# Attention product with the values as the stationary operand, in a hybrid encoder layer on one core

## The reference, cut to what matters

```python
def window_sink_attention(q, k, v, sinks):
    ...
    scores = jnp.einsum('bnqkgd,bnskd->bnkgqs', q, k_band).astype(jnp.float32) * (ATT_HEAD_DIM ** -0.5)
    scores = jnp.where(valid[None, :, None, None, None, :], scores, -jnp.inf)
    sink = sinks.astype(jnp.float32).reshape(1, 1, ATT_KV_HEADS, ATT_GROUP, 1)
    lse = jnp.logaddexp(jax.nn.logsumexp(scores, axis=-1), sink)
    probs = jnp.exp(scores - lse[..., None]).astype(v.dtype)
    out = jnp.einsum('bnkgqs,bnskd->bnqkgd', probs, v_band)
    return out.reshape(b, s, ATT_Q_W)

def hybrid_mixer(h, w_in, b_in, w_qk_conv, b_qk_conv, sinks, g_att, g_ml, w_out):
    ...
    att = rmsnorm(att, g_att)
    ml = rmsnorm(ml.reshape(b, s, ML_HEADS, ML_V_DIM), g_ml.reshape(ML_HEADS, ML_V_DIM)).reshape(b, s, ML_V_W)
    return jnp.concatenate([att, ml], axis=-1) @ w_out
```

## Time and profile before

| what | value |
|---|---|
| median of 3 runs | 1009.53 us (1009.29 to 1009.66) |
| profiled execution | 1009.17 us |
| its span | 1007.4 us |
| PE busy | 997.8 us, 99% of the span |
| DVE, ACT, POOL busy | 744.7, 505.8, 25.9 us |
| granted TensorE clock | 0.999 of full speed, mean |

### The profile page before, as it was taken

The page is one execution under the profiler, slowest core; times in us unless marked ns, Lnnn a source line. Parts: engine busy times, 40 slices in busy tenths (PEclk is TensorE's granted clock), DMA queues, the critical chain, the costliest instruction groups (busy, mean ns, idle before and its releaser), DMA issues.

```text
span 1007.4 us, 13062 instructions
## 1 busy us (share of the span) xinstructions
PE 997.8 (99%) x4807; PEld 823.8 (82%) x4807; DVE 744.7 (74%) x1164; ACT 505.8 (50%) x949; POOL 25.9 (3%) x40
## 2 busy tenths in 40 slices
PE   9999999999999999999999999999999999999997
PEld 6788888888888888788888888888888888888886
DVE  4563678875645569997777777777776879996796
ACT  5663448643733225755445445445544634444573
POOL 2000000000300000000000000000000000000000
PEclk9999999999999999999999999999999999999999
DMA  9527554222832241423223223223222999035104
GB/s 343 186 91 224 187 189 168 85 66 108 298 117 84 84 124 51 141 84 105 63 84 104 63 84 104 63 84 100 68 81 81 391 363 336 1 117 190 40 1 167
DMA packets 93255, 133.97 MB, mean 133 GB/s; under 512 B 5884, under 2 KB 56188, under 8 KB 93192
## 3 DMA queue, kind: packets, MB, share of 16 engines
q1 hardware_dynamic: 92808, 132.98, 39.5%
q0 software_dynamic: 96, 0.00, 0.1%
q10 hardware_dynamic: 288, 0.15, 0.1%
HBM read 104.75 MB, written 28.35 MB: 132 GB/s over the span
## 4 chain that ended last, share of the span: by engine, by line
PE 77%; DVE 4%; issue 1%; ACT 0%; DVEq 0%; ACTq 0%
PE pz L2339 7%; PE pz L2340 7%; PE pz L2338 7%; PE pd L2338 6%; PE pd L2339 6%; PE pd L2340 6%; PE pd L2359 4%; PE pd L2362 4%; PE pd L2361 4%; PE pz L2359 3%; PE pz L2362 3%; PE pz L2361 3%; PE pd L2243 3%; PE pd L2245 3%; PE pd L2244 3%; PE pz L2274 1%
## 5 line engine op out<-in xcount | busy, mean ns | idle before, releaser
L1109 ACT ACTIVATE ws_hi<-raw 128x512 fp32r<-128x512 f32 x88 | 52.9, 626 | 102.4 <-PE pz L2340 48.0
L2338 PE MATMUL pz<-ht_hi,ws_hi 128*128 128x512 f32 x240 | 93.7, 390 | 0.2 <-ACT u L1131 0.2
L2340 PE MATMUL pz<-ht_hi,ws_lo 128*128 128x512 f32 x240 | 93.5, 389 | 0.0
L2339 PE MATMUL pz<-ht_lo,ws_hi 128*128 128x512 f32 x240 | 93.4, 389 | 0.0
L2338 PE MATMUL pd<-ht_hi,ws_hi 128*128 128x512 f32 x200 | 78.0, 390 | 0.5 <-DVE u L1792 0.5
L2340 PE MATMUL pd<-ht_hi,ws_lo 128*128 128x512 f32 x200 | 77.9, 389 | 0.0
L2339 PE MATMUL pd<-ht_lo,ws_hi 128*128 128x512 f32 x200 | 77.9, 389 | 0.0
L1809 DVE SCALAR_TENSOR_TENSOR gate<-u,vec,gate 128x1023 f32<-128x1023 f32 (+1 forms) x44 | 56.4, 1283 | 19.4 <-ACT gate L1151 18.6
L1779 DVE TENSOR_TENSOR ws_lo<-raw,ws_hi 128x512 fp32r<-128x512 f32 x88 | 58.5, 686 | 0.8 <-ACT ws_hi L1109 0.7
L1809 DVE SCALAR_TENSOR_TENSOR lift<-u,vec,lift 128x1023 f32<-128x1023 f32 (+1 forms) x44 | 56.2, 1278 | 0.1
L1184 ACT ACTIVATE d_hi<-a 128x512 fp32r<-128x512 f32 x44 | 27.7, 631 | 54.4 <-PE pd L2362 29.6
(11 more groups left out here) (312 smaller groups left out, 2550.8 us busy)
## 6 DMA issues: line engine op xcount, KB each, us to landing
raw<-in_w_up SPq DMA_DIRECT2D x48, 512.0 KB, 5.0
b<-in_w_down SPq DMA_DIRECT2D x49, 256.0 KB, 7.0
act_rows<-gate SPq DMA_DIRECT2D x22, 512.0 KB, 2.6
a<-act_rows SPq DMA_DIRECT2D x44, 256.0 KB, 4.7
w_raw<-in_w_wide SPq DMA_DIRECT2D x16, 512.0 KB, 3.9
x_turned<-in_x_t SPq DMA_DIRECT2D x8, 512.0 KB, 9.5
x_in<-in_x SPq DMA_DIRECT2D x8, 512.0 KB, 12.9
wo_hi_rows<-wo_new_hi SPq DMA_DIRECT2D x8, 512.0 KB, 5.0
```

The lines of the kernel that those rows point to most:

```text
L1109: nc.scalar.activation(ws_hi[m][:, :, :], summand(p, i), ACT.Copy).then_inc(s["ws_hi_made"], 1)
L2338: mm(dst, wh[:, k, :], xh[:, k, :], start=begins and k == 0, stop=False, skip_group_check=not begins)
L2339: mm(dst, wh[:, k, :], xl[:, k, :], start=False, stop=False, skip_group_check=not begins)
L2340: ins = mm(dst, wl[:, k, :], xh[:, k, :], start=False, stop=k == KH - 1, skip_group_check=not begins)
```

## The change

The values become the stationary operand (`v[0:kw, rows]`, 64 columns for each of the two groups) and the transposed probabilities the moving one, 256 columns: two matmuls a chunk in place of four, each writing one half of the partitions. The result lies with features on the partitions and needs no transpose before the output projection. Since queries now lie on the free axis, the probabilities are divided by their sum before they are transposed. ACT squares a chunk's result in two halves, DVE adds them down to 64 columns a chunk, a product with ones sums over the partitions, and the inverse root (`att_root`, `att_norm`, at tile 1 of the loop over tiles, now on 128x256 where it was 128x16) goes to DRAM as a row and comes back spread over the partitions (`store_att_row` at tile 2, `spread_att_row` at tile 3); DVE scales by it, one tile of 128 tokens at a time (`att_scale`: tiles 0 and 1 at the loop's end, the others in the output projection). The product with ones (`att_total`) stands behind `ml_sum(0)`.

```diff
@@ SP
-            load_gate(1)
             for i in range(NT):
+                if i == NT - 1:
+                    sp.wait_ge(s["att_scaled"], NT)
+                    load_gate(1)
@@ ACT
             def att_square(n):
                 act.wait_ge(s["att_kept"], n + 1)
-                if n == 0:
-                    act.wait_ge(s["att_scored"], 5)
-                else:
-                    act.wait_ge(s["att_squared"], n)
-                nc.scalar.activation(att_squares[:, :, :], zq[:, n, :, :], ACT.Square,
-                                     accum_out=sq_att[:, n:n + 1]).then_inc(s["att_squared"], 1)
+                act.wait_ge(s["att_sq_added"], 2 * n)
+                for h, dst in enumerate((att_sq_a, att_sq_b)):
+                    last = nc.scalar.activation(dst[:, :, :], zq[:, n, 2 * h:2 * h + 2, :], ACT.Square)
+                last.then_inc(s["att_squared"], 1)
...
-                    for m in (n - 5, n - 4):
-                        if n % 2 == 1 and 0 <= m < NC:
-                            att_square(m)
+                    if 0 <= n - 5 < NC:
+                        att_square(n - 5)
...
             def mix_high(i):
+                act.wait_ge(s["att_scaled"], i + 1)
+                nc.scalar.activation(mix_hi[i % 2][:, 0:4, :].rearrange("p j (n t) -> p n j t", n=2),
+                                     zq[:, 2 * i:2 * i + 2, :, :], ACT.Copy).then_inc(s["mix_hi_made"], 1)
                 act.wait_ge(s["mix_turned"], i + 1)
-                nc.scalar.activation(mix_hi[i % 2][:, :, :].rearrange("p k t -> p (k t)"), pz[1][:, :], ACT.Copy)\
+                nc.scalar.activation(mix_hi[i % 2][:, 4:NK, :].rearrange("p k t -> p (k t)"), bank[2], ACT.Copy)\
                     .then_inc(s["mix_hi_made"], 1)
+            def att_root():
+            def store_att_row():
+                act.wait_ge(s["att_norm_step"], 3)
+                act.dma_start(att_r_d.rearrange("(g t) -> g t", g=4), att_r[0:P:32, :]).then_inc(s["rows_stored"], 16)
+            def spread_att_row():
+                act.wait_ge(s["rows_stored"], 48)
+                act.dma_start(att_row[:, :], att_r_d.partition_broadcast(P)).then_inc(s["rows_spread"], 16)
-            def att_scale(n):
@@ DVE
             def att_sum(n):
...
+                nc.vector.reciprocal(inv[:, n % 4, :], total1[:, u, :]).then_inc(s["att_summed"], 1)
+                dve.wait_ge(s["att_summed"], 3 * n + 2)
+                p = probs[:, u, :, 0:kw]
+                nc.vector.tensor_tensor(p, p, inv[:, n % 4, :].unsqueeze(2).to_broadcast([P, 4, kw]), ALU.mult)\
+                    .then_inc(s["att_summed"], 1)
             def att_keep(n):
+                nc.vector.tensor_copy(zq[:, n, :, :], bank[7][:, c:c + 256].rearrange("p (j t) -> p j t", j=4))\
+            def att_sq_add(n):
+                dve.wait_ge(s["att_squared"], n + 1)
+                nc.vector.tensor_tensor(att_sq_a[:, :, :], att_sq_a[:, :, :], att_sq_b[:, :, :], ALU.add)\
+                    .then_inc(s["att_sq_added"], 1)
+                dve.wait_ge(s["att_sq_added"], 2 * n + 1)
+                nc.vector.tensor_tensor(z[:, AK, n * CHUNK:(n + 1) * CHUNK], att_sq_a[:, 0, :], att_sq_a[:, 1, :], ALU.add)\
+                    .then_inc(s["att_sq_added"], 1)
...
                     if n in (8, 10):
                         scale_q((n - 8) // 2)
+                    if 0 <= n - 6 < NC:
+                        att_sq_add(n - 6)
...
             def att_norm():
-                nc.vector.reciprocal(r_att[:, :], r_att0[:, :]).then_inc(s["att_norm_step"], 1)
+                nc.vector.reciprocal(att_r[:, :], att_r[:, :]).then_inc(s["att_norm_step"], 1)
+            def att_scale(i):
+                nc.vector.tensor_tensor(v, v, r, ALU.mult).then_inc(s["att_scaled"], 1)
@@ PE
             def turn_probs(n):
-                pe.wait_ge(s["att_exped"], n + 1)
+                pe.wait_ge(s["att_summed"], 3 * n + 3)
             def attend(n):
-                for j in range(4):
-                    kv = j // 2
-                    ins = mm(bank[7][:, c + j * HD:c + (j + 1) * HD], probs_t[0:kw, n % 2, j, :],
-                             v[0:kw, kv * HD:(kv + 1) * HD], start=True, stop=True)
+                for kv in range(KV_HEADS):
+                    rows = slice(kv * HD, (kv + 1) * HD)
+                    ins = mm(bank[7][rows, c:c + 4 * CHUNK], v[0:kw, rows],
+                             probs_t[0:kw, n % 2, 2 * kv:2 * kv + 2, :].rearrange("k u t -> k (u t)"), start=True, stop=True)
...
+            def att_total():
+                pe.wait_ge(s["att_sq_added"], 2 * NC)
+                for g in range(4):
+                    ins = mm(bank[2][32 * g:32 * g + 32, 0:2 * P], ones[:, :], z[:, AK, g * 2 * P:(g + 1) * 2 * P],
             def turn_mix(i):
-                for n in (2 * i, 2 * i + 1):
-                    for kv in range(2):
-                        dst = pz[1][:, 2 * kv * P:(2 * kv + 2) * P].rearrange("p (a t) -> p a t", a=2)
-                        c = (n % 2) * CHUNK
-                        nc.tensor.transpose(dst[:, :, c:c + CHUNK],
-                                            zq[:, n, 2 * kv:2 * kv + 2, :].rearrange("p j d -> p (j d)"), ident[:, :])
```

More of the change, by code:

```diff
@@ L320, in hymba_kernel @@
         ident = sb("ident", [P, P])
-        fold = sb("fold", [P, P])
+        ones = sb("ones", [P, 32])
+        att_sq_a = sb("att_sq_a", [P, 2, CHUNK])
         gates_t = sb("gates_t", [P, 2, NT, ML_HEADS])
@@ L376, in hymba_kernel @@
             att_scored att_topped att_exped att_summed att_v_turned att_v_made
[L377 removed]
+            att_p_turned att_p_made att_done att_kept att_squared att_sq_added dve_step
             ml_scored ml_k_turned wide_used wide_done wide_kept wide_gated ml_summed ml_stated
@@ L532, in load_wo @@
                 if k < 4:
-                    kv, a = k // 2, k % 2
-                    for pp in range(2):
-                        r = (kv * 4 + 2 * pp + a) * HD
-                        sp.dma_start(wo_raw[u][pp * HD:(pp + 1) * HD, :], w_out_d[r:r + HD, :]).then_inc(wo_loaded[u], 16)
+                    for kv in range(KV_HEADS):
+                        r = (kv * 4 + k) * HD
+                        sp.dma_start(wo_raw[u][kv * HD:(kv + 1) * HD, :], w_out_d[r:r + HD, :]).then_inc(wo_loaded[u], 16)
                 else:
@@ L771, in _ @@
             nc.gpsimd.memset(reset[:, 0:S:P], 0.0).then_inc(s["const_made"], 1)
-            for n, off in enumerate((0, 64, -64)):
-                if n:
-                    pool.wait_ge(s["const_made"], 2 + n)
-                nc.gpsimd.affine_select(out=fold[:, :], in_=fold[:, :], compare_op=ALU.not_equal, fill=1.0,
-                                        base=off, pattern=[[-1, P]], channel_multiplier=1)\
-                    .then_inc(s["const_made"], 1)
             nc.gpsimd.affine_select(out=pair_rows[0:ML_HEADS, :, :].rearrange("h r (e d) -> h r e d", e=2),
@@ L1013, in _ @@
             for i in range(NT):
-                if i == 0:
-                    act.wait_ge(s["att_norm_step"], 1)
-                    nc.scalar.activation(r_att0[:, :], att_sums[:, :], ACT.Sqrt, bias=eps[:, :],
-                                         scale=1.0 / (ATT_HEADS * HD)).then_inc(s["att_norm_step"], 1)
-                    for n in range(4):
-                        att_scale(n)
+                if i == 1:
+                    att_root()
+                if i == 2:
+                    store_att_row()
+                if i == 3:
+                    spread_att_row()
                 if i == NT - 2:
@@ L1026, in _ @@
                         ml_scale(i - NT + 4)
-                    for n in (2 * i + 2, 2 * i + 3):
-                        att_scale(n)
             def h2_high(i):
@@ L1593, in ml_carry @@
                 dve.wait_ge(s["ml_stated"], i + 1)
-                if i == 0:
-                    nc.vector.tensor_copy(att_sums[:, :], bank[7][:, HALF - NC:]).then_inc(s["att_norm_step"], 1)
                 if i:
@@ L1728, in _ @@
                     ml_carry(i + 1)
-                if i == 0:
+                if i == 1:
                     att_norm()
+                if i >= NT - 3 and i < NT - 1:
+                    att_scale(i - NT + 3)
                 if i in (2, 3):
@@ L1740, in _ @@
                     mix_scale(i + 2)
+                    att_scale(i + 2)
                 if i == NT - 1:
@@ L2136, in beside @@
                     if n >= 0 and n % 2 == 0:
-                        if n == NC:
+                        if 0 <= n - 4 < NC:
+                            attend(n - 4)
+                        if 0 <= n - 2 < NC:
                             turn_probs(n - 2)
-                        for m in (n - 4, n - 3):
-                            if 0 <= m < NC:
-                                attend(m)
-                        if 0 <= n - 2 < NC and n != NC:
-                            turn_probs(n - 2)
+                        if 0 <= n - 3 < NC:
+                            attend(n - 3)
```

(11 more changed lines are left out.)

57 lines of the change are left out of this document (30 added, 27 removed).

## The result

| what | before | after |
|---|---|---|
| median of the runs beside each other | 1009.6 us | 1024.97 us (1023.91 to 1026.28) |
| ratio, 95% interval | | 1.0149 (1.0137 to 1.0161) |
| profiled execution, its span | 1009.17, 1007.4 us | 1023.91, 1022.2 us |
| granted TensorE clock, mean | 0.999 | 0.992 |

What follows compares the result with a forecast made beforehand. PE was busy 99%, with DVE and ACT also near their limit in attention. 13.9 + 1.5 + 1.1 + 0.2 - 3.5 = +13.2 on the profiled 1009.2 gave 1022.4, forecast 1022; own range 1017 to 1027, wider range 1013 to 1028.

Steps and rivals of the forecast that it cites:

- copy of step 8: DVE's copy opening the four attention blocks: to end at about 161.0 us, 0.7 later than before.
- PE's loss of work: `attend` on PE from 0.865 to 0.5 us a chunk, 5.8 us less for 16 chunks.
- DVE's gain: Added DVE work in attention: product, dependent inverse, two additions, 1.25 us a step, 2.5 a block.
- The walk over the blocks: Steps 8 to 16, copy to copy, with ACT and DVE waits: 72.8 us against 58.9 before, +13.9.
- 0.7 back for the last pair of `attend`: Behind the four blocks, 0.7 us returns, leaving +13.9 us at the last wide units.
- Rival 3: PE's clock falls while PE stands in the four blocks: 0 to 2 us a block, 1022 to 1030, taken 1026; 9%.
- a granted clock under 1: Listed sign that the forecast is wrong; the profile before ran at 0.999.
- The tail: Behind attention: last additions and squares +1.5 us, 256-column inverse +1.1, two `att_scale` +0.2.
- Rival 1: ACT's wait is hidden, blocks together 60.1 us: 1009.7 us, or 1011 to 1015 if part shows; 13%.
- Rival 2: PE's saving lands in full: 1000.5 us, needing 1.25 us idle in DVE in every step; 7%.
- Rival 4: The norm's row through DRAM comes late and `att_scale(0)` stops DVE and the loop: 1024 to 1028 us; 3%.
- The output projection: `turn_mix` loses four transposes a tile, 0.44 us each tile, 3.5 us for 8.

Runs made afterwards that it cites:

- sq_later: The kernel after, with ACT's squares of a chunk placed one step later, same instructions: 1014.95 us, ratio 1.0051.
- pool_adds: The kernel after, with the two additions of each chunk's squares on GpSimd in place of DVE: 1015.01 us, ratio 1.0043.
- ones_set: The kernel after without ACT's squares and DVE's additions, ones set once in their place (a bound only, no norm taken): 1009.85 us, ratio 1.0003.
- later_turn: The kernel after with ACT's squares a step later and PE's transpose of the odd chunk one wide unit later: 1010.94 us, ratio 1.0005.
- pool_cont: After with GpSimd additions, later odd transpose, last two squares in step 19, 8-column inverse from neighbouring columns, single values to DRAM: 1021.28 us.
- pool_keep: After with additions on GpSimd, odd transpose later, last two chunks' squares in step 19, bank 7 copy on ACT: 1005.85 us, ratio 0.9961.
- all_small: After with squares a step later, odd transpose later, last three chunks' squares and additions in step 19, 8-column inverse (strided squares stationary): 1014.04 us.
- pool_all: After with additions on GpSimd, odd transpose later, last chunks' squares and additions in step 19, 8-column inverse (strided squares stationary): 1011.18 us.

## Why the prediction came out as it did

- **The forecast.** 1022 was forecast and 1024.97 measured; the mechanism that carried it, ACT's squares waiting inside the step, is the one that sq_later, pool_adds and ones_set confirm from three sides. On the spans, 13.2 us were forecast and 1.09 (way to the copy of step 8) + 13.69 + 1.04 + 2.65 - 3.67 = 14.8 measured. The terms below say where the 1.6 between them lie; of the 3.0 us between the two times the other 1.4 are the rounding of 1022.4 to 1022 and the median of after, 1.06 us above its profiled execution.
- **PE's loss of work.** `attend` was taken at 0.5 us and is 0.58, the upper end that the state products of 129 columns gave. It cost nothing here, since DVE is later.
- **DVE's gain.** Sum, inverse and product were taken at 1.1 us from start to start and are 167.94 - 166.92 = 1.02; the additions at 0.5, measured 0.46.
- **The walk over the blocks.** 21.0, 17.5, 17.95, 16.3 were predicted, 20.85, 17.04, 17.71, 17.03 measured: 72.8 against 72.63 us. The copy of step 8, predicted to end at 161.0, ended at 161.4. ACT's standstill is 2.9 to 4.9 us a step, at least 2.8 was said. PE's one wait for `w_lo` at step 10 is 2.1 us, where 3 to 4 was said.
- **Behind the blocks: the step that was mis-sized.** "0.7 back for the last pair of `attend`" was predicted, so that the last wide units would be 13.9 late. They are 15.8 late: the stretch took 27.19 us, 1.04 more than before, so this term is off by 1.7. The clock is the reason. Rival 3 had this right ("0 to 2 us a block"), at 9%, as an alternative to the forecast and not as a part of it, and the prediction itself had named a granted clock under 1 as a sign of being wrong. In most blocks DVE's lateness covers it, as their sum without any term for the clock shows; in the last stretch, where PE is the late engine, nothing does. Four kernels have the same 120 records of PE in this stretch and wait the same 0.8 us there. In sq_later they keep PE busy for 24.8 us at a clock of 1.00, in after and in ones_set for 26.4 us at 0.94 (stretches of 27.19 and 27.22 us), in pool_adds for 27.6 us at 0.88. ones_set has neither squares nor additions, so the 1.6 us between 25.63 and 27.2 are the clock's and not the loop's.
- **The tail.** +2.8 was predicted (1.5 + 1.1 + 0.2), +2.65 measured. By parts, from the starts on DVE: to the first `den` behind the last `wide_keep` it takes 264.22 - 260.51 = 3.71 us in place of 2.83, so the additions cost 0.9 where 1.5 was said (29.68 - 28.82 = 0.86 by pool_adds, which has none on DVE). The tile with the inverse takes 272.02 - 267.62 = 4.40 us in place of 3.55: 0.85 where 1.1 was said, since DVE had idle time in that tile to give for it (0.68 us in before, none in after). The last two tiles, with the two `att_scale`, take the other 0.9, where 0.2 was said: the first product costs 0.3, the second its full 0.6 (288.86 to 289.46). Errors of opposite sign made the sum look better than its parts, which is luck. The inverse itself was predicted from a slope at 1.56 us and took 1.66 from start to start (1.75 long). The 2.1 us, estimated in the prediction from the Trainium skill ("VectorE: DVE Perf Modes", section "First, the fixed hardware budget"), is too much.
- **Rival 1** (1009.7), the wait hidden, did not occur: ACT stood in every step of the blocks. Where the squares' place hides it, sq_later and later_turn take 1014.95 and 1010.94 us. **Rival 2** (1000.5) was not reached: the fastest version stands 5.4 us over it. **Rival 4** did not occur in after (row stored and spread by 284.01 us, where `att_scale(0)` came without a wait) and was made to occur in pool_cont.
- **The output projection.** -3.5 predicted, 14.8 - 18.5 = -3.7 measured (span against the last `ml_t`).

## What to carry to other kernels

When work is split between two engines in one step, ask for each new wait which instruction of the other engine it stands behind, and whether that one waits for the first engine in the same step; if it does, the two take turns, and shifting one of the two by a step added no instruction and gave back 10 us here. A faster product on the engine that bounds the kernel is worth nothing as long as the others reach their limit with what was moved to them: here the saving showed only when additions and transposes had found other places (1007.34 us), and more of it with the copy moved too (1005.85). And look at a kernel stretch by stretch before judging a variant, since a loss at its end can hide that the rest of it works.

## What was not expected of the hardware

- **The stride of the stationary operand.** 128 columns with 32 bytes between them: 3.86 us for eight fp32 matmuls of one column; with neighbouring columns 1.84 us, 0.48 against 0.23 us each. The Trainium skill ("SBUF — State Buffer", section "Door 1: The DMA port swizzle") says that accesses that leave a line of 16 bytes pay a penalty; the trace agrees in direction, and adds a factor of two for this load.
- **DVE beside GpSimd.** In after the first `att_scale` takes 1.47 us and the other ones 0.68. GpSimd ran this row then:

```profile
283.66 1.28 POOL L795 TENSOR_TENSOR mixed<-ml_t,ml_gate 128x512 f32<-128x512 f32 x1 [2.12 <-DVE ml_t L1644]
```

It ends at 284.94, and 0.54 us later DVE's product is done, as if it had stood until then. In pool_keep the taps beside GpSimd's additions take 1.48 us in place of 1.28, and one product of the probabilities 0.89 in place of 0.69:

```profile
179.66 0.47 POOL L793 TENSOR_TENSOR att_sq_a<-att_sq_a,att_sq_b 128x128 f32<-128x128 f32 x1 [3.59 <-ACT att_sq_b L944]
```

```profile
179.79 0.89 DVE L1495 TENSOR_TENSOR probs<-probs,inv 128x512 f32<-128x512 f32 x1
```

The Trainium skill (the same page, section "SBUF: two separate sides") says that a DVE instruction with two SBUF inputs and a GpSimd instruction that reads SBUF lock each other out for the whole instruction. The rows agree, and it is a price of the additions on GpSimd: 0.2 us where they meet.
- **The clock.** In after it fell behind four waits of PE of 2.15 to 2.60 us (163.18 - 162.75 = 0.43 us a matmul), but not behind one of 2.07 us (step 10). In sq_later it stayed at 1.00 behind waits of 2.69 and 3.01 us, in ones_set it fell behind one of 1.72. So the length of one wait does not tell whether the clock falls. In all_small and pool_all it fell behind 3.86 us of matmuls of one column without any wait. In before PE never waited over 0.6 us between 100 and 380 us, and its clock stayed at 1.00 there.
